# First block of a two-block layer stack: the order of turning, scoring and the fourth input product, and the place of two modulation rows on VectorE

## The chip, the cores and the metric

The kernel runs on one core of one Trainium2 chip. The metric is the device time of one execution in microseconds (us), as the median of several runs. Three runs of the kernel before took 3032.94, 3033.38 and 3045.9 us; the median is 3033.38 us.

## What is computed

The reference is two blocks, each of two layers, on 256 tokens of width 1024. The change touches only the attention part of the first block, in both of its layers:

```python
mod = (c_act @ w_ada[l] + b_ada[l])[:, None, :]
shift1, scale1, gate1, shift2, scale2, gate2 = jnp.split(mod, 6, axis=-1)
h = rms_norm(x, norm1_g[l]) * (1.0 + scale1) + shift1
z = h @ w_in[l]          # q 512, k 128, v 128, conv_x/b/c 3*256, pool_x 256
q = partial_rope(rms_norm(q, q_norm_g[l]), cos, sin)
k = partial_rope(rms_norm(k, k_norm_g[l]), cos, sin)
attn_o = windowed_gqa(q, k, v, attn_sink[l])       # 8 query heads, 2 key heads, a sink
conv_o = conv_b * short_conv(conv_c * conv_x, conv_w[l])
pooled = multiscale_pool(pool_x)
pool_o = jnp.einsum('bsgc,gce->bsge', pooled, pool_w[l]).reshape(b, s, POOL_WIDTH) * pool_scale[l]
mix = jnp.concatenate([attn_o, conv_o, pool_o], axis=-1) @ w_out[l]
x = x + gate1 * mix
h2 = rms_norm(x, norm2_g[l]) * (1.0 + scale2) + shift2
x = x + gate2 * peer_ffn(...)       # 16384 experts: most of the first block's time
```

The second block (three kinds of attention and an MLP, two layers) follows, and is not touched.

## The kernel before

Each engine has a program of its own, written out by hand. The engines meet at semaphores: `wait_ge` stands in an engine's queue, and all that is queued behind it on that engine waits too. All data are float32. The 256 tokens are two tiles (t) of 128 partitions.

**The input product** z = h @ w_in is cut into four slabs of weights, `in0` (queries), `in1` (keys, values, first conv part), `in2` (the rest of conv) and `in3` (the 256 columns of pooling), each a product on TensorE (PE) into one of the two halves of the PSUM tensor `acc` and then copied out by ScalarE (ACT) with `keep_acc`. The halves of `acc` are dealt out in the fixed order of the list `ACCS_A` (line 174), and a use waits until the use before it in the same half has been copied out. The order is in0, in1, in2, in3, sc0, sc1, sc2, sc3, then out0 and so on.

**Ahead of attention.** VectorE (DVE) normalizes and rotates queries and keys (lines 2594 to 2605) as soon as in0 and in1 are copied out, while PE is still at `in2`. PE runs `gemm_T` of in2 (line 1186, timed at L973), the product in3 (lines 1187 to 1195, L1193), and then turns q0, q1 and k (transposes, L1027), which ACT copies to SBUF (in the second layer DVE copies q1). Then come `score(0)` (L1096), the pooling product `pool0` (L1210), `score(1)`, and `pool1` (L1221), which needs ACT's copy of pool0.

**Attention** goes over four groups g of heads. For each: `score(g)` on PE; `masked(g)` on DVE (scale and mask out of PSUM L2450, maximum L2455, and three small operations); `exps(g)` on ACT (L1783, L1785); `turn_probs(g)` on PE (L1107) in two halves, one copied by ACT and one by DVE in `sums(g)` (L2472, L2474, and the copy at L1658); `values(g)` on PE (L1122); `attended(g)` on DVE (L2501), which frees the bank. DVE does masked(0), masked(1), and then for each g: sums(g), masked(g + 2) while there is one (for g = 2 `convolved()` instead, L2615 to L2625), attended(g). ACT runs pool1's scaling (L1863), exps(1), and then for each g its half of the copy and exps(g + 2).

**Rows of modulation.** In the first layer the 12 pieces of 512 columns of c_act @ w_ada are not all computed at the start. `ada_first(s)` on DVE (L2415, L2422) adds up one of them from four loaded pieces in eight operations on 128x512, and PE sums the partitions with a product by ones, `ada_added(s)` (L1137). ada_first(3) and ada_first(4) stand behind the rotation and ahead of masked(0). PE takes their sums, ada_added(3) and (4), only after values(3), and their results are needed after the output product.

**Loads.** SyncE (SP) issues all weight loads, in this order: slab in3, the pieces of rows 3 and 4, slabs out0 and out1, the pieces of rows 5, 6, 7, slab wq0 and so on. A piece of row s waits until the same piece of row s - 1 has been used by DVE (`ada_used`, L685). The load of out1 waits for in3's product to be done.

After attention PE runs ada_added(3), ada_added(4), the turns `mix0` and `mix1` of the attention output, and the output product out0 (L952).

Of the kernel before, what the change touches and what calls it, by code (L numbers as in the profile page):

```python
# [19 lines left out]
T = S // P  # L20
# [136 lines left out]
def spread(ap, axis, n):  # L157
# [13 lines left out]
         + [f"br{c}" for c in range(NB)] + ["wo0", "wo1"] + [f"up{i}" for i in range(8)]  # L171
         + [f"dn{i}" for i in range(8)],
}
ACCS_A = [f"in{i}" for i in range(4)] + [f"sc{i}" for i in range(4)]
ACCS_A += ["out0", "out1", "wq0", "s0", "wq1", "s1", "wq2", "s2", "wq3", "s3"]
ACCS = {
    "a": (["ada2", "ada3", "ada0", "ada1"] + ACCS_A, ACCS_A),
    "b": ["dq", "dk", "sc0", "dv", "sc1", "mq", "sc2", "mk", "sc3", "mv", "sc4", "misc0", "sc5", "misc1",
# [62 lines left out]
def two_blocks(nc, io, out):  # L241
    ctx = ExitStack()
    with ctx:
        def sem(name):
            return ctx.enter_context(nc.semaphore(name))
# [47 lines left out]
        qk_ready = Signal(sem("qk_ready"), a=1, b=4)  # L293
# [158 lines left out]
        z = ra.take(T, D)  # L452
# [156 lines left out]
        def qpair(t, j):  # L609

            return z[:, t, j * P:j * P + P]
# [335 lines left out]
        def _(pe):  # L947
# [28 lines left out]
            def gemm_T(block, l, use):  # L976
                w = w8(block, use)
                pe.wait_ge(*slabs.full_at(block, l, use))
                pe.wait_ge(*accs.free_at(block, l, use))
                for j in range(4):  # L980
                    ins = columns_T(acc[:, accs.buf(block, use), j, :], w, hT, j * P)
                ins.then_inc(accs.full_sem(block, use), 1)
# [39 lines left out]
            def turn(block, l, use, blocks, rows=P):  # L1022

                ring, bank = turned_bank(block, use)
                pe.wait_ge(*ring.free_at(block, l, use))
                for i, src in enumerate(blocks):
                    ins = pe.transpose(bank[0:rows, i * P:i * P + P], src, ident[:])  # L1027
                ins.then_inc(ring.full_sem(block, use), 1)
# [55 lines left out]
            def wait_turned(block, l, *uses):  # L1084

                for u in uses:
                    pe.wait_ge(*(probs if u in PROBS[block] else turns).emptied_at(block, l, u))

            def score(block, l, g):
                d = group(block, g)  # L1090
                use = f"sc{g}"
                pe.wait_ge(*accs.free_at(block, l, use))
                b = accs.buf(block, use)
                for hh in range(2):
                    for t in range(T):
                        ins = pe.matmul(acc[:, b, 2 * hh + t, :], d["q"](hh, t), d["k"](hh), start=True, stop=True)  # L1096
                ins.then_inc(accs.full_sem(block, use), 1)
# [35 lines left out]
            for l in range(DEPTH):  # L1133
# [49 lines left out]
                if l == 0:  # L1183
                    ada_added(1, prob_ps[:, 0])
                    ada_added(2, prob_ps[:, 1])
                gemm_T("a", l, "in2")
                pe.wait_ge(*slabs.full_at("a", l, "in3"))
                pe.wait_ge(*accs.free_at("a", l, "in3"))
                w = w8("a", "in3")
# [4 lines left out]
                                        start=(k == 0), stop=(k == KD - 1))  # L1194
                ins.then_inc(accs.full_sem("a", "in3"), 1)

                pe.wait_ge(*qk_ready.at("a", l, 1))
                for n in range(2):
                    turn("a", l, f"q{n}", [qpair(t, 2 * n + c) for c in range(2) for t in range(T)])
                turn("a", l, "k", [z[:, t, 512:640] for t in range(T)])  # L1200
                wait_turned("a", l, "q0", "q1", "k")
                score("a", l, 0)

                pe.wait_ge(*accs.emptied_at("a", l, "in3"))
                pe.wait_ge(*turns.free_at("a", l, "pool0"))
                pooled = turn_ps[:, turns.buf("a", "pool0"), :].rearrange("p (c s) -> p c s", c=2)
# [3 lines left out]
                        ins = pe.matmul(pooled[r:r + 64, g // 2, :], z[:, kt, 768 + 64 * g:832 + 64 * g],  # L1210
                                        pool_m[:, kt, g, :], start=(kt == 0), stop=(kt == 1))
                ins.then_inc(turns.full_sem("a", "pool0"), 1)
                score("a", l, 1)
                pe.wait_ge(*turns.emptied_at("a", l, "pool0"))
                pe.sem_inc(passed["pe"], 1)
                pe.wait_ge(*turns.free_at("a", l, "pool1"))
# [200 lines left out]
                else:  # L1417
# [3 lines left out]
                    with pe.Fori(0, 12) as it:  # L1421
                        for j in range(8):
                            i = it * 8 + (PLAIN + 3 + j)
# [211 lines left out]
        def keep_turned(eng, block, l, use, dst, rows=P, n=512):  # L1635

            ring, bank = turned_bank(block, use)
            eng.wait_ge(*ring.full_at(block, l, use))
            src = bank[0:rows, 0:n]
            if len(dst.shape) == 3:  # L1640
                src = src.rearrange("p (k s) -> p k s", k=dst.shape[1])
            copy(eng, dst, src).then_inc(ring.free_sem(block, use), 1)
# [75 lines left out]
        def _(act):  # L1718
# [9 lines left out]
            def keep_acc(block, l, use, *pairs):  # L1728

                act.wait_ge(*accs.full_at(block, l, use))  # L1730
                for dst, src in pairs[:-1]:
                    act.copy(dst, src)
                act.copy(*pairs[-1]).then_inc(accs.free_sem(block, use), 1)
# [4 lines left out]
            def whole(block, use):  # L1738
                return acc[:, accs.buf(block, use)]
# [38 lines left out]
            def exps(block, l, g):  # L1778

                act.wait_ge(*sm_ready.at(block, l, g + 1))  # L1780
                s = sm_of(block)
                if block == "a":
                    act.activation(esink[:, g % 2], esink[:, g % 2], ACT.Exp)  # L1783
                for u in range(4):
                    ins = act.activation(s[:, g % 2, u], s[:, g % 2, u], ACT.Exp, bias=nm[:, g % 2, u:u + 1],  # L1785
                                         accum_out=den[:, g % 2, u:u + 1])
                ins.then_inc(p_ready.sem, 1)
# [36 lines left out]
            for l in range(DEPTH):  # L1824
# [25 lines left out]
                    for s in (1, 2):  # L1850
                        ada_copied(s, mod_flat[:, 512 * ADA_ORDER[s]:512 * ADA_ORDER[s] + 512], prob_ps[:, (s - 1) % 2])
                keep_acc("a", l, "in2", (zT[:, 2:6], whole("a", "in2")))
                keep_acc("a", l, "in3", (z[:, :, 768:1024], whole("a", "in3")[:, 0:2]))
                keep_turned(act, "a", l, "q0", qT[:, 0:2])
                if l == 0:
                    keep_turned(act, "a", l, "q1", qT[:, 2:4])
                keep_turned(act, "a", l, "k", kT, n=S)
                keep_turned(act, "a", l, "pool0", plT)
                exps("a", l, 0)
                act.wait_ge(*turns.full_at("a", l, "pool1"))  # L1860
                pooled = turn_ps[:, turns.buf("a", "pool1"), :].rearrange("p (c s) -> p c s", c=2)
                for c in range(2):
# [474 lines left out]
        def _(dve_):  # L2337
# [84 lines left out]
            def ada_first(s):  # L2422

                for p in range(4):
                    if p == 0:
                        if s >= 3:
                            dve.wait_ge(ada_out, s - 2)
                        dve.wait_ge(bias_row_in, 16 * s)
                    ada_piece(s, p, start_pieces, ada_acc[:, s % 2], bias_row)
                dve.drain().then_inc(ada_sum, 1)  # L2430
# [13 lines left out]
            def masked(block, l, g):  # L2444

                d, s, use = group(block, g), sm_of(block), f"sc{g}"
                dve.wait_ge(*accs.full_at(block, l, use))
                b = accs.buf(block, use)
                for hh in range(2):
                    ins = dve.scalar_tensor_tensor(s[:, g % 2, 2 * hh:2 * hh + 2].rearrange("p t s -> p (t s)"),  # L2450
                                                   acc[:, b, 2 * hh:2 * hh + 2].rearrange("p t s -> p (t s)"), d["scale"],
                                                   d["mask"](hh).rearrange("p t s -> p (t s)"), ALU.mult, ALU.add)
                ins.then_inc(accs.free_sem(block, use), 1)
                dve.drain()
                dve.tensor_reduce(mx, s[:, g % 2], X, ALU.max)  # L2455
                dve.drain()
                if block == "a":
                    sink = spread(sinks.rearrange("p (hh j) -> p j hh", hh=2)[:, g], 2, T)
                    mx2, es2, nm2 = (v.rearrange("p (hh t) -> p hh t", t=T) for v in (mx, esink[:, g % 2], nm[:, g % 2]))
                    dve.tensor_tensor(mx2, mx2, sink, ALU.max)  # L2460
                    dve.drain()
                    dve.tensor_scalar(nm[:, g % 2], mx, -1.0, None, ALU.mult)
                    dve.drain()
                    dve.tensor_tensor(es2, nm2, sink, ALU.add).then_inc(sm_ready.sem, 1)
                else:
                    dve.tensor_scalar(nm[:, g % 2], mx, -1.0, None, ALU.mult).then_inc(sm_ready.sem, 1)
# [80 lines left out]
            for l in range(DEPTH):  # L2547
# [55 lines left out]
                dve.drain()  # L2603
                rt = [rope_t[:, i].rearrange("p t (h e) -> p t h e", e=8) for i in range(4)]
                rotate(heads[:, :, :, 0:8], heads[:, :, :, 8:16], cosA, sinA, rt).then_inc(qk_ready.sem, 1)
                if l == 0:
                    ada_first(3)
                    ada_first(4)
                else:
                    keep_turned(dve, "a", l, "q1", qT[:, 2:4])  # L2610

                def convolved():
# [13 lines left out]

                masked("a", l, 0)
                masked("a", l, 1)
                for g in range(4):
                    sums("a", l, g)  # L2630
                    if g + 2 < 4:
                        masked("a", l, g + 2)
                    elif g == 2:
                        convolved()
                    attended("a", l, g)
# [161 lines left out]
                else:  # L2797
# [6 lines left out]
                    with dve.Fori(0, 12) as it:  # L2804
                        for j in range(8):
                            i = it * 8 + (PLAIN + 3 + j)
# [365 lines left out]
```

## Time and profile before

| | |
|---|---|
| median of three runs | 3033.38 us |
| the profiled execution | 3034.02 us, span 3032.2 us |
| mean granted TensorE clock | 0.987 |
| first layer, from the start of in3 to the start of out0 | 84.0 to 131.6 us |
| second layer, the same | 1120.0 to 1164.5 us |

The profile shows one execution. Times in the trace are counted from the start of the span. A row of a timeline has start, duration, engine, line and operation, output and input with shapes, the number of instructions merged into it, and in brackets how long the engine was idle before it and what released it. The granted clock is 1.00 at 2.4 GHz and 0.50 at 1.2 GHz.

### The profile page before, as it was taken

What the parts mean: (1) busy time and instruction counts of PE and PEld (TensorE: products, weight loads), DVE (VectorE), ACT (ScalarE), POOL (GpSimd) and SP (SyncE); (2) the same over time, 40 slices, a digit from 0 to 9 for tenths busy, and PEclk for the clock granted to TensorE, in tenths of its full rate; (3) what the DMA queues carried; (4) which work ended last, traced back from release to release, by engine and by line L of the source; (5) the groups of instructions that cost most, each with busy time, mean ns of one, the idle gap of its engine ahead of it and who ended that gap; (6) DMA issues with size and microseconds to landing.
All of it is one profiled execution on the core that took longest, in us unless ns stands there. A gap on an engine that the chain in (4) does not pass through costs nothing.

```text
span 3032.2 us, 49210 instructions
## 1 busy us (share of the span) xinstructions
PE 2937.6 (97%) x17378; PEld 2555.9 (84%) x17378; DVE 1970.5 (65%) x3639; ACT 1308.6 (43%) x2110; POOL 274.5 (9%) x398
## 2 busy tenths in 40 slices
PE   8899999999999999999999999998999999999999
PEld 4686989999999876887999999998977888878897
DVE  4759966777777633898666666666556654655664
ACT  1245834444444412575444444444443433533433
POOL 0026700000000000572000000000000000000000
PEclk9899999999999998999999999999999999999999
DMA  8542256666666641404555555554334454324454
GB/s 327 197 157 84 72 187 235 226 235 232 227 234 230 206 155 56 167 8 128 192 186 186 198 191 194 190 194 176 125 120 168 171 185 172 147 112 160 153 181 153
DMA packets 130815, 524.41 MB, mean 173 GB/s; under 512 B 17981, under 2 KB 28093, under 8 KB 108025
## 3 DMA queue, kind: packets, MB, share of 16 engines
q1 hardware_dynamic: 120648, 508.13, 48.4%
q10 hardware_dynamic: 10034, 14.52, 1.4%
q8 instruction: 81, 1.33, 0.2%
q14 instruction: 52, 0.43, 0.0%
HBM read 519.44 MB, written 3.16 MB: 172 GB/s over the span
## 4 chain that ended last, share of the span: by engine, by line
PE 86%; DVE 7%; ACT 4%; issue 1%; DVEq 1%; DMA 1%; ACTq 0%; POOL 0%; SPq 0%
PE acc L1390 23%; PE prob_ps L1378 21%; PE acc L1014 7%; PE acc L1603 6%; PE acc L1616 6%; PE acc L999 3%; PE acc L973 2%; PE acc L1550 2%; PE acc L1360 2%; PE turn_ps L1122 2%; PE acc L952 2%; PE prob_ps L1341 2%; PE acc L1575 1%; PE acc L1096 1%; PE acc L1253 1%
## 5 line engine op out<-in xcount | busy, mean ns | idle before, releaser
L1378 PEld LDWEIGHTS prob_ps<-hTr,utr 128*128 128x128 f32 x5472 | 686.3, 191 | 19.6 <-issue 2.0
L1378 PE MATMUL prob_ps<-hTr,utr 128*128 128x256 f32 x5472 | 692.3, 283 | 1.3 <-issue 1.1
L1390 PE MATMUL acc<-vr,wtr 128*128 128x512 f32 x2736 | 663.6, 391 | 0.2 <-DVE vr L2776 0.2
L1390 PEld LDWEIGHTS acc<-vr,wtr 128*128 128x128 f32 x2736 | 499.3, 188 | 94.9 <-issue 0.6
L2776 DVE TENSOR_TENSOR vr<-slab,vr 128x1024 fp32r<-128x1024 f32 x228 | 279.3, 1225 | 357.9 <-ACT vr L2036 357.9
L2036 ACT CAST vr<-slab 128x1024 fp32r<-128x1024 f32 x228 | 239.5, 1050 | 524.1 <-PE acc L1390 524.0
L2751 DVE TENSOR_TENSOR utr<-slab,utr 128x1024 fp32r<-128x1024 f32 x228 | 277.9, 1219 | 16.1 <-ACT utr L2003 16.1
L2305 POOL TENSOR_TENSOR small<-small 128x1 f32<-128x1 f32 (+4 forms) x29 | 26.2, 902 | 2610.3 <-DVE small L2368 1410.5
L2003 ACT CAST utr<-slab 128x1024 fp32r<-128x1024 f32 x228 | 238.6, 1047 | 16.6 <-DMA slab<-in_peer_u 10.5
L3032 DVE TENSOR_TENSOR slab_lo<-slab,w_hi 128x2048 fp32r<-128x2048 f32 x64 | 143.8, 2288 | 123.0 <-ACT w_hi L2271 123.0
L2271 ACT CAST w_hi<-slab 128x2048 fp32r<-128x2048 f32 x64 | 119.3, 1907 | 158.5 <-DMA slab<-in_pack_b 150.6
L2027 ACT ACTIVATE arena<-prob_ps 128x256 f32<-128x256 f32 x228 | 87.6, 384 | 194.1 <-PE prob_ps L1378 194.1
L2857 DVE TENSOR_TENSOR slab_r<-slab,arena_r 128x2048 fp32r<-128x2048 f32 (+1 forms) x52 | 115.7, 2258 | 84.5 <-ACT arena_r L2123 84.4
L973 PE MATMUL acc<-hT,slab 128*128 128x256 f32 x704 | 157.7, 379 | 2.9 <-ACT hT L1652 2.9
L1616 PE MATMUL acc<-w_hi,uTr 128*128 128x512 f32 x512 | 157.8, 389 | 2.3 <-issue 2.3
L2328 POOL TENSOR_SCALAR slab<-iota,arena 128x128 f32<-128x128 f32 x256 | 152.2, 609 | 45.0 <-ACT arena L1658 30.5
L2740 DVE TENSOR_SCALAR slab<-iota,arena 128x128 f32<-128x128 f32 x512 | 152.7, 367 | 1.2
L973 PEld LDWEIGHTS acc<-hT,slab 128*128 128x128 f32 x704 | 131.5, 190 | 21.1 <-issue 3.7
L1360 PEld LDWEIGHTS acc<-slab 128*128 128x128 f32 x1024 | 121.7, 192 | 19.1 <-DVE slab L2744 15.7
L1360 PE MATMUL acc<-slab 128*128 128x128 f32 x1024 | 127.1, 277 | 6.9 <-ACT slab L1984 4.2
L2415 DVE SCALAR_TENSOR_TENSOR arena<-arena,small 128x512 f32<-128x512 f32 x152 | 113.8, 749 | 15.7 <-DMA arena<-in_pack_a 7.4
L1014 PE MATMUL acc<-arena_r,hT_hi 128*128 128x512 f32 (+2 forms) x320 | 122.3, 382 | 0.0
(314 smaller groups left out, 4415.4 us busy)
## 6 DMA issues: line engine op xcount, KB each, us to landing
slab<-in_pack_b SPq DMA_DIRECT2D x132, 1024.0 KB, 4.8
slab<-in_peer_v SPq DMA_DIRECT2D x256, 512.0 KB, 3.5
slab<-in_peer_u SPq DMA_DIRECT2D x244, 512.0 KB, 4.5
arena<-in_pack_a SPq DMA_DIRECT2D x84, 512.0 KB, 4.8
slab<-in_pack_a SPq DMA_DIRECT2D x40, 1024.0 KB, 6.9
arena<-in_peer_u SPq DMA_DIRECT2D x6, 1024.0 KB, 15.1
slab<-in_pack_b SPq DMA_DIRECT2D x4, 832.0 KB, 5.6
arena<-in_pack_a SPq DMA_DIRECT2D x2, 1024.0 KB, 18.6
```

What stands on the lines that cost most here:

```text
L973: ins = pe.matmul(dst, w(k, a, P), lhs[:, k, :], start=(k == 0), stop=(k == KD - 1))
L1014: ins = pe.matmul(dst[:, t, 0:n], hT_r[hp][:, 4 * h + k, t * P:t * P + P], proj_operand(u0 + h, wp)[:, k, a:a + n], start=(h == 0 and k == ...
L1360: ins = pe.matmul(gate_ps[:, n % 2, q * P:q * P + P], rows[:, n % 2, 1, q, :], rows[:, n % 2, 0, q, :], start=True, stop=True)
L1378: ins = pe.matmul(prob_ps[:, m % 2, 0:S], utr[:, m % 2, uh, k * P:k * P + P], hTr[:, hh, k, :], start=(k == 0 and n == 0), stop=(k == KD - ...
L1390: ins = pe.matmul(y_ps[:, t, n, :], wtr[:, m % 2, wh, t * P:t * P + P], v[:, vh, n * 512:n * 512 + 512], start=first and k == 0, stop=last ...
L1603: ins = pe.matmul(acc[:, accs.buf("b", use), 2 * h + j, :], mlp_operand(u, wp)[:, k, j * P:j * P + P], hm_r[hp][:, k, :], start=(k == 0 an ...
L1616: ins = pe.matmul(acc_nat(accs.buf("b", f"dn{n}"))[:, t, :], uTr[:, up, 4 * j + k, t * P:t * P + P], mlp_operand(u, wp)[:, k, :], start=(j ...
L2003: act.copy(utr[:, m % 2, 0], expert_u[:, m % 2]).then_inc(ut_act.sem, 1)
L2036: act.copy(v_place(l, i)[:, 0], v_raw(l, i, m)).then_inc(v_hi.sem, 1)
L2740: dve.tensor_scalar(rows[:, n % 2, 0, q, :], iota[:], pairsT[:, 0, tok:tok + 1], pairsT[:, 2, tok:tok + 1], ALU.is_equal, ALU.mult)
L2751: dve.tensor_tensor(utr[:, m % 2, 1], expert_u[:, m % 2], utr[:, m % 2, 0].bitcast(F32), ALU.subtract).then_inc(ut_dve.sem, 1)
L2776: dve.tensor_tensor(v_hl[:, 1], v_raw(l, i, m), v_hl[:, 0].bitcast(F32), ALU.subtract)\
```

## The change

On PE, turning q0, q1 and k and score(0) move ahead of the product in3, and score(1) moves ahead of pool0. The order of the halves of `acc` follows: sc0 now comes ahead of in3. On ACT, exps(0) moves ahead of the copy of in3 and of pool0. This holds for both layers. On DVE, in the first layer only, ada_first(3) moves behind masked(1) and ada_first(4) behind masked(3).

```diff
-ACCS_A = [f"in{i}" for i in range(4)] + [f"sc{i}" for i in range(4)]
+ACCS_A = ["in0", "in1", "in2", "sc0", "in3"] + [f"sc{i}" for i in range(1, 4)]
...
                 gemm_T("a", l, "in2")
+                pe.wait_ge(*qk_ready.at("a", l, 1))
+                for n in range(2):
+                    turn("a", l, f"q{n}", [qpair(t, 2 * n + c) for c in range(2) for t in range(T)])
+                turn("a", l, "k", [z[:, t, 512:640] for t in range(T)])
+                wait_turned("a", l, "q0", "q1", "k")
+                score("a", l, 0)
+
                 pe.wait_ge(*slabs.full_at("a", l, "in3"))
                 pe.wait_ge(*accs.free_at("a", l, "in3"))
...
                 ins.then_inc(accs.full_sem("a", "in3"), 1)
 
-                pe.wait_ge(*qk_ready.at("a", l, 1))
-                for n in range(2):
-                    turn("a", l, f"q{n}", [qpair(t, 2 * n + c) for c in range(2) for t in range(T)])
-                turn("a", l, "k", [z[:, t, 512:640] for t in range(T)])
-                wait_turned("a", l, "q0", "q1", "k")
-                score("a", l, 0)
-
+                score("a", l, 1)
                 pe.wait_ge(*accs.emptied_at("a", l, "in3"))
...
                 ins.then_inc(turns.full_sem("a", "pool0"), 1)
-                score("a", l, 1)
                 pe.wait_ge(*turns.emptied_at("a", l, "pool0"))
...
                 keep_acc("a", l, "in2", (zT[:, 2:6], whole("a", "in2")))
-                keep_acc("a", l, "in3", (z[:, :, 768:1024], whole("a", "in3")[:, 0:2]))
                 keep_turned(act, "a", l, "q0", qT[:, 0:2])
                 if l == 0:
                     keep_turned(act, "a", l, "q1", qT[:, 2:4])
                 keep_turned(act, "a", l, "k", kT, n=S)
+                exps("a", l, 0)
+                keep_acc("a", l, "in3", (z[:, :, 768:1024], whole("a", "in3")[:, 0:2]))
                 keep_turned(act, "a", l, "pool0", plT)
-                exps("a", l, 0)
...
-                if l == 0:
-                    ada_first(3)
-                    ada_first(4)
-                else:
+                if l:
                     keep_turned(dve, "a", l, "q1", qT[:, 2:4])
...
                 masked("a", l, 0)
                 masked("a", l, 1)
+                if l == 0:
+                    ada_first(3)
                 for g in range(4):
                     sums("a", l, g)
                     if g + 2 < 4:
                         masked("a", l, g + 2)
+                        if l == 0 and g == 1:
+                            ada_first(4)
                     elif g == 2:
                         convolved()
                     attended("a", l, g)
```

## Rows read from the trace of the kernel before

**Rows 1.** The page: busy time of the engines; the last chain by engine.

```profile
PE 2937.6 (97%) x17378; PEld 2555.9 (84%) x17378; DVE 1970.5 (65%) x3639; ACT 1308.6 (43%) x2110; POOL 274.5 (9%) x398
PE 86%; DVE 7%; ACT 4%; issue 1%; DVEq 1%; DMA 1%; ACTq 0%; POOL 0%; SPq 0%
```

**Rows 2.** The chain that ended last, first layer: start, us, what.

```profile
94.51 0.75 DVE arena L2415
...
95.45 0.69 DVE arena L2450
...
108.47 1.71 PE prob_ps L1107 x8
```

**Rows 3.** Timeline, first layer, PE and ACT.

```profile
84.04 7.07 PE L1193 MATMUL acc<-slab,hT 128*128 128x256 f32 x32
84.24 1.01 ACT L1733 COPY arena<-acc 128x1024 f32<-128x1024 f32 x1 [13.23 <-PE acc L973]
...
90.94 1.04 PE L1027 MATMUL turn_ps<-ident,arena 128*128 128x128 f32 x8
91.14 0.59 ACT L1733 COPY arena<-acc 128x512 f32<-128x512 f32 x1 [5.89 <-PE acc L1193]
91.62 1.49 ACT L1658 COPY arena<-turn_ps 128x512 f32<-128x512 f32 x3
...
93.37 1.14 PE L1096 MATMUL acc<-arena 64*128 64x256 f32 x8 [0.67 <-ACT arena L1658]
94.44 2.00 PE L1210 MATMUL turn_ps<-arena 128*64 128x256 f32 x16
...
101.08 1.18 PE L1107 MATMUL prob_ps<-ident,arena 128*128 128x128 f32 x8 [2.55 <-issue]
...
126.69 3.19 PE L1137 MATMUL prob_ps<-arena,small 128*128 128x512 f32 x4
...
129.71 1.04 PE L1027 MATMUL turn_ps<-ident,arena 128*128 128x128 f32 x8
...
131.58 13.97 PE L952 MATMUL acc<-slab,arena 128*128 128x512 f32 x32 [0.83 <-ACT arena L1658]
```

**Rows 4.** Timeline, first layer, DVE.

```profile
81.82 6.57 DVE L2415 SCALAR_TENSOR_TENSOR arena<-arena,small 128x512 f32<-128x512 f32 x8
...
98.69 1.28 DVE L2450 SCALAR_TENSOR_TENSOR arena<-acc,arena 128x512 f32<-128x512 f32 x2
...
115.48 0.48 DVE L2501 TENSOR_TENSOR arena<-turn_ps,small 128x128 f32<-128x128 f32 x2
...
116.78 0.68 DVE L2615 TENSOR_TENSOR arena<-arena 128x512 f32<-128x512 f32 x1
...
120.15 0.69 DVE L2625 TENSOR_TENSOR arena<-arena 128x512 f32<-128x512 f32 x1
...
126.93 0.49 DVE L2501 TENSOR_TENSOR arena<-turn_ps,small 128x128 f32<-128x128 f32 x2 [2.87 <-PE turn_ps L1122]
```

**Rows 5.** Windows of 1 us, first layer; the granted clock follows the engines.

```profile
101.00:102.00 1.00, 0.92 (x8) 0.85 (x8) 0.78 (x4) 0.70 (x2) 0.00 (x0) 0.94 0.98 412
...
129.00:130.00 1.00, 1.00 (x5) 0.43 (x4) 0.00 (x0) 0.42 (x2) 0.00 (x0) 0.90 0.00 0
```

**Rows 6.** Timeline, second layer, PE.

```profile
1119.97 7.07 PE L1193 MATMUL acc<-slab,hT 128*128 128x256 f32 x32
...
1136.53 1.09 PE L1107 MATMUL prob_ps<-ident,arena 128*128 128x128 f32 x8 [0.20 <-ACT arena L1785]
...
1139.93 1.97 PE L1122 MATMUL turn_ps<-arena 128*128 128x64 f32 x16 [1.24 <-ACT arena L1658]
...
1157.42 3.65 PE L1122 MATMUL turn_ps<-arena 128*128 128x64 f32 x16
...
1164.50 16.83 PE L952 MATMUL acc<-slab,arena 128*128 128x512 f32 x32 [0.83 <-issue]
```

**Rows 7.** SP's queue, first layer: issue of out0 and out1.

```profile
88.94 3.50 SPq L668 DMA_DIRECT2D slab<-in_pack_a  x4
```

## The prediction

> **What bounds the kernel now.** I read the page first: PE is busy 97% of the span and holds 86% of the chain that ended last; DVE holds 7% [rows 1]. A move can win only where that chain leaves PE, so I followed the chain through the attention of both layers of the first block. In the first layer it lies on DVE's modulation rows until 95.26, and then on masked(0) at 95.45 [rows 2]. There the reader is to see the target: DVE is through with the rotation at 81.82 and spends the 13.63 us to 95.45 on two rows of two times eight operations [rows 2, 4], and only then masks scores that PE finished at 94.51 (93.37 + 1.14) [rows 3]. So before the change the rows cost at most 0.94 us: that is how late masked(0) is behind its scores. The timelines of PE, ACT and DVE then give the durations, and the windows the clock: TensorE stands at 2.4 GHz up to 101.9 us, drops to 1.2 GHz inside the window at 101, just behind PE's idle stretch of 2.55 us, and is back for good inside the window at 129, with one return in between [rows 3, 5].
>
> **PE's new order, first layer.** PE is free at 84.04 [rows 3]; the queries have been ready since 81.8, so the turns start at once. ACT must first copy in2 (84.24, 1.01 us); a next copy starts 0.11 us before the one ahead of it ends (91.14 + 0.59 against 91.62) [rows 3], so with the hand-over the copy of q0 starts at about 85.15. From that copy's start to score(0) took 1.75 us (91.62 to 93.37) and takes it again: score(0) at 86.9, next work 1.07 later at 87.97, then in3, 6.90 us (84.04 to 90.94): score(1) starts at 94.87 and is done at 96.01 [rows 3]. masked(0) then starts at 88.04, 7.4 us earlier, and with exps(0) is wholly hidden beside in3. But masked(1) waits for score(1) at 96.03, where it started at 98.69 [rows 4]: only **2.66 us** of the 7.4 reach the next step. DVE is idle for about 6 us ahead of score(0) and 4.8 between masked(0) and score(1), and the rows are no longer there to use it.
>
> **PE's stalls.** pool1 now follows pool0 with no score between, so PE waits for ACT's copy (about 0.6 us with the hand-over, from the copies in rows 3). turn_probs(0) can start at about 99.5 instead of 101.08 [rows 3]. That gain dies at once: values(0) needs DVE's half of the copy, in sums(0), which is queued behind ada_first(3).
>
> **DVE's new order, first layer.** From 96.03 DVE has, end to end: three masks of 3.24 us (95.45 to 98.69) = 9.72 [rows 2, 4]; two rows of 6.81 (13.63 / 2) = 13.62; four sums and three attended, of which one pair takes 1.30 (115.48 to 116.78) and attended alone about 0.40, = 4.80; the convolution 4.06 (116.78 to 120.84) = 4.06 [rows 4]. That is 32.20 us: 128.2. What can make it wait? attended(0) finds values(0) done. masked(3) waits for score(3): PE can start the second half of values(0) at 107.0, and at 1.2 GHz needs 1.83 (half of the 3.65 of a values group), 1.71 for the turn and twice 1.07 for the score [rows 2, 3, 6]: 112.6, against DVE ready at 111.5, so 1.1 us; at 2.4 GHz nothing. I take the slow clock, since the trace had it at this place, from 101.9 on [rows 5]: **129.3**. Then the second half of values(3), 1.83 us: PE is through at 131.1, where it was at 126.69 [rows 3]. Where 13.6 us of rows were nearly free, they now stand in the chain, less the waits that DVE had in attention and the 2.66 us.
>
> **From there to out0.** ada_added(3) and (4) are four passes of 512 columns; one takes 13.97 / 32 = 0.43 us at 2.4 GHz, twice that at 1.2, so 3.4 us (before, with the clock rising within them, 3.02: 126.69 to 129.71). The two turns take 1.04 at 2.4 GHz or twice that, then 0.83 of wait [rows 3]. With the clock back at the turns, out0 starts at 136.4, with it back after them at 137.3; before it was 131.58. That is +4.8 or +5.7, and I take **+5.2**. Bounds: all of it at 2.4 GHz gives 128.2 + 1.0 + 1.7 + 1.0 + 0.8 = 132.7, +1.2; a clock that comes back only within out0, as in the second layer, where out0 took 16.83 instead of 13.97 us [rows 3, 6], gives +5.7 + 2.9 = +8.6.
>
> **Second layer.** It has no rows to move. PE is free for the turns at 1119.97 [rows 6]. By the same steps: q0's copy at 1121.08, score(0) at 1122.8, in3 to 1130.8, score(1) to 1131.9, pool0 to 1133.9, the copy 0.6, pool1 to 1135.5, gain2 to 1137.4: turn_probs(0) starts 0.9 us later than 1136.53 [rows 6]. masked(0) was not late here for DVE's sake; ACT's exps(0) ended 0.2 us before PE took it up, so starting it 6 us earlier is worth 0.2. exps(1) stands on ACT behind the copy of gain2, which follows PE: values(0) at 1140.4 instead of 1139.93 [rows 6]. The rest follows in step: **+0.5**, between 0 and +0.9 without the clock. The clock may fall one step later, because the dense product in3 ends 4 us later: up to 1.7 us back.
>
> **What moves at no cost.** SP: the pieces of row 4 now wait for ada_first(3)'s, so the loads of out0 and out1, issued from 88.94 [rows 7], go out at about 106.1. 17 us later, but out0 is needed at 136.4: cover of 30 us. The pieces of row 5 wait for ada_first(4) (115.5 to 122.3) and are needed by ada_first(5) after the mix turns, some 13 us later. out1's load waits for in3's product, later by 4 us, with the same cover. in3 waits for in2's copy in its half of acc, done at 85.3; score(1) waits for masked(0)'s read, done at 89.3. The exp table load on ACT goes with exps(0) into the idle time beside in3.
>
> **Sum.** +5.2 + 0.5 = +5.7 on the profiled 3034.02 us, which is 0.64 above the median of the runs: 3039.1 us; I say 3039.
>
> **Rivals.**
> 1. *The clock holds* (not slower). The change takes away the idle stretch ahead of turn_probs(0), just where the clock fell [rows 3, 5]. If it then stays at 2.4 GHz, the first layer costs +1.2; if the second layer's attention too stays fast, values fall from 3.65 to 1.97 us three times and out0 from 16.83 to 13.97 [rows 6], some 8 to 10 us with the turns. That gives 3025 to 3034. Against it: ada_first(3) opens new idle stretches on PE, about 2 and 2.5 us around the first half of values(0), and ada_first(4) one of some 4 us ahead of the second half of values(2). The Trainium skill, "TensorE: Matmul & The Clock Gate", Part 1, has it that dense work releases the throttle and gaps bring it back; by it the dense stretch moved to 95 us speaks for this case and the new gaps against it. [...]
> 2. *The clock is lost for longer*: low until within out0, +8.6 and +0.9: 3043.
> 3. *out0's weights come late* (slower by over 0.5%). Their load would have to take over 30 us from its issue at 106; each further us is a us. 15 us more would be needed to reach 3049.
> 4. *The change does as its order suggests*: DVE's idle time swallows the rows. In attention DVE waited some 9.0 us in all between 102 and 127, in eight places, the largest the 2.87 us ahead of attended(3) [rows 4]. 13.6 - 2.66 - 9.0 leaves 1.9 even if every wait were filled, and the last one can't be, since values(3) itself must run: it is the case of 3035 to 3036, not a gain.
>
> **Chances.** Forecast (3036.5 to 3042) 0.57; rival 1, 0.14; rival 2 (3042 to 3046), 0.16; rival 3, 0.03; rival 4, 0.10. Range 3031 to 3046.5: it takes in the slow-clock bound and the upper half of rival 1, leaving out some 0.15. A measurement of this kernel tells about 0.5% (15 us) from no change: that is 3018 to 3048.5. Nearly all cases lie within it: same 0.93, slower 0.05, faster 0.02.
>
> **What would show it.** After, in the first layer: masked(0) near 88 and masked(1) near 96; ada_first(3) from 99 to 106 with PE idle; values(0) finished near 109; ada_first(4) near 115.5 to 122; values(3) ending near 131 and out0 starting near 137. The chain there should lie on L2415 again, for 13 us, now within attention. out0's slab should be issued near 106 with no wait of PE for it. Second layer: turn_probs(0) about 0.9 us later against in3's old start. Wrong would be: a clock at 1.00 from 102 to 112; masked(1) well before 96; PE waiting for a DMA at out0.

## The result

| | before | after |
|---|---|---|
| median, 20 runs each | 3035.32 us | 3042.15 us |
| profiled execution | 3034.02 us | 3039.9 us |
| span | 3032.2 us | 3038.1 us |

The changed kernel is slower by a little: the ratio is 1.0023, with a 95% interval of 1.0015 to 1.0032, or 4.6 to 9.7 us. That is within the 0.5% that the prediction took as the least it could tell from no change; 20 runs of each kernel tell more. The forecast was 5.7 us more than before; measured are 6.8 between the medians and 5.9 between the two profiled executions. Executions in a slower state (two of the twelve of e5, for one) are left out of all ratios. The page counts the same instructions and the same busy time of PE to 0.1 us as before [rows 1]. The 5.9 us between the spans are therefore time in which PE stood idle.

The page of the changed kernel:

```profile
PE 2937.6 (97%) x17378; PEld 2555.5 (84%) x17378; DVE 1970.8 (65%) x3639; ACT 1309.2 (43%) x2110; POOL 275.4 (9%) x398
```

The timeline of the changed kernel, first layer, PE:

```profile
84.17 1.04 PE L1027 MATMUL turn_ps<-ident,arena 128*128 128x128 f32 x8
...
87.02 1.14 PE L1096 MATMUL acc<-arena 64*128 64x256 f32 x8 [0.66 <-ACT arena L1658]
88.09 7.17 PE L1200 MATMUL acc<-slab,hT 128*128 128x256 f32 x32
...
95.19 1.14 PE L1096 MATMUL acc<-arena 64*128 64x256 f32 x8
...
100.19 1.09 PE L1107 MATMUL prob_ps<-ident,arena 128*128 128x128 f32 x8
...
107.51 1.97 PE L1122 MATMUL turn_ps<-arena 128*128 128x64 f32 x8 [2.63 <-DVE arena L1658]
...
124.41 1.97 PE L1122 MATMUL turn_ps<-arena 128*128 128x64 f32 x8 [3.44 <-DVE arena L1658]
...
137.45 10.97 PE L952 MATMUL acc<-slab,arena 128*128 128x512 f32 x25 [0.83 <-ACT arena L1658]
```

And DVE of the same stretch, with SP's issue of out0 and out1 (L1200 and L1211 are now the lines of in3 and pool0):

```profile
88.20 1.29 DVE L2450 SCALAR_TENSOR_TENSOR arena<-acc,arena 128x512 f32<-128x512 f32 x2 [6.15 <-PE acc L1096]
...
96.39 1.29 DVE L2450 SCALAR_TENSOR_TENSOR arena<-acc,arena 128x512 f32<-128x512 f32 x2 [4.87 <-PE acc L1096]
...
99.69 6.59 DVE L2415 SCALAR_TENSOR_TENSOR arena<-arena,small 128x512 f32<-128x512 f32 x8
...
106.82 2.62 SPq L668 DMA_DIRECT2D slab<-in_pack_a  x4
...
112.89 1.29 DVE L2450 SCALAR_TENSOR_TENSOR arena<-acc,arena 128x512 f32<-128x512 f32 x2 [0.55 <-PE acc L1096]
...
116.19 6.60 DVE L2415 SCALAR_TENSOR_TENSOR arena<-arena,small 128x512 f32<-128x512 f32 x8
```

The reader is to see two things. DVE waits 6.15 us ahead of masked(0) and 4.87 us ahead of masked(1), where it had work before [rows 4]. Then it does 6.6 us of row 3 (99.69 to 106.28) ahead of sums(0), while PE gets through the first half of values(0), and 6.6 us of row 4 ahead of attended(1) and sums(2). Twice PE's values stop half done for DVE's half of the copy (2.63 us in values(0), 3.44 us in values(2)). Before, the first layer's stretch from PE free of in2 to the start of out0 was 131.58 - 84.04 = 47.54 us [rows 3]; now it is 137.45 - 84.17 = **53.28 us**. That stretch is the measure of the experiments.

### The profile page after: what moved, and what is told of

Its sections match the earlier page's. It is cut to its first block, busy times and chain, and to the rows that moved or that the text cites. A ratio compares the mean times of both kernels' runs of the same rounds, so it can differ in the third digit from the quotient of the medians.

```text
span 3038.1 us, 49210 instructions
## 1 busy us (share of the span) xinstructions
PE 2937.6 (97%) x17378; PEld 2555.5 (84%) x17378; DVE 1970.8 (65%) x3639; ACT 1309.2 (43%) x2110; POOL 275.4 (9%) x398
## 4 chain that ended last, share of the span: by engine, by line
PE 87%; DVE 6%; ACT 3%; issue 1%; DMA 1%; DVEq 1%; ACTq 0%; SPq 0%; POOL 0%
PE acc L1390 23%; PE prob_ps L1378 22%; PE acc L1014 7%; PE acc L1603 6%; PE acc L1616 6%; PE acc L999 3%; PE acc L973 3%; PE acc L1550 2%; PE acc L1360 2%; PE acc L952 2%; PE turn_ps L1122 2%; PE prob_ps L1341 2%; PE acc L1575 1%; PE acc L1096 1%; DMA arena<-in_pack_a 1%
```

## The experiments

The stretch is read from one profiled execution of each kernel, between two starts of PE's rows in its timeline. The ratio is over many executions (12 of each experiment), against runs of the kernel before taken beside them. The edit of e2 is shown against the kernel before, the others against the changed kernel.

| kernel | stretch, us | ratio to before (95% interval) |
|---|---|---|
| before, before_again | 47.54, 47.35 | |
| after, after_again | 53.28, 52.92 | 1.0023 (1.0015 to 1.0032) |
| e1_order_only | 55.19 | 1.0022 (1.0012 to 1.0032) |
| e2_rows_only | 54.60 | 1.0015 (1.0003 to 1.0026) |
| e4_thin_rows | 44.50 | 0.9989 (0.9978 to 1.0000) |
| e3_fill, e3_again | 38.44, 44.62 | 0.9993 (0.9981 to 1.0006), 1.0003 (0.9991 to 1.0015) |
| e5_both_scores | 46.81 | 0.9994 (0.9982 to 1.0005) |
| e6_order_pe | 49.70 | none: one run, 3042.70 us, against one of before, 3033.12 us |

before_again and after_again are one run each too (3042.34 and 3043.92 us). The 20 runs of the kernel before lie between 3028.93 and 3045.9 us, so a single run says nothing of a difference of some us.

### e4: the moved rows without their length

Here n is 8 for rows 3 and 4: the other 504 columns of these two rows are left out, so this kernel only serves to measure.

```diff
-    ins = dve.scalar_tensor_tensor(total, pieces[:, p, k], ...
+    ins = dve.scalar_tensor_tensor(total[:, 0:n], pieces[:, p, k, 0:n], ...
```

> The changed kernel with rows 3 and 4 computed for 8 of their 512 columns only (the rest of these two rows is left out): the same instructions, waits and loads, without their length. Theory: each row falls from 6.8 to about 1.5 us, and 10.6 us leave DVE's chain, of which PE gives back some: stretch 44 to 46 us. Rival (the loads and waits that hang on the rows, or the order, cost): the stretch stays above 50 us. Total: theory 5 to 9 us below the changed kernel.

The stretch fell from 53.28 to 44.50 us, and the ratio to before from 1.0023 to 0.9989: 0.34%, some 10 us, where 5 to 9 were expected. Waits, loads and order are those of the changed kernel; only the length of the rows on DVE is gone. So in this place the length of the rows costs 8.8 us of the stretch, and neither their loads nor their waits do. That another place is cheaper in the same order is for e3 to show.

### e2: the rows moved, the order as before

ada_first(4) stands behind masked(3).

```diff
-                if l == 0:
-                    ada_first(3)
-                    ada_first(4)
-                else:
+                if l:
                     keep_turned(dve, "a", l, "q1", qT[:, 2:4])
...
                 masked("a", l, 1)
+                if l == 0:
+                    ada_first(3)
```

> The old order on PE and ACT, with the two rows behind masked(1) and masked(3). Theory: masked(0) starts at 94.5 with its scores, masked(1) at 97.8, 1.4 us later than in the changed kernel, and the whole chain of DVE follows it: stretch 54 to 55 us, total 6 to 9 us above before. Rival (the order is the cost): stretch about 48 us, total as before.

The stretch is 54.60, as the theory had it. The whole is 1.0015, or 4.6 us with an interval of 0.9 to 7.9, against 6 to 9 expected. The timeline of e2 on DVE shows the shift:

```profile
94.58 1.29 DVE L2450 SCALAR_TENSOR_TENSOR arena<-acc,arena 128x512 f32<-128x512 f32 x2 [12.63 <-PE acc L1096]
97.82 1.28 DVE L2450 SCALAR_TENSOR_TENSOR arena<-acc,arena 128x512 f32<-128x512 f32 x2
101.11 6.61 DVE L2415 SCALAR_TENSOR_TENSOR arena<-arena,small 128x512 f32<-128x512 f32 x8
```

DVE idles for 12.63 us, and masked(0) starts only 0.87 us earlier than the 95.45 of before [rows 2]. In the old order the rows had held up the masks by 0.9 us where they were.

### e1 and e6: the order alone

Both rows go back ahead of the masks, and none stands behind masked(1) or masked(3).

```diff
                 rotate(heads[:, :, :, 0:8], ...).then_inc(qk_ready.sem, 1)
+                if l == 0:
+                    ada_first(3)
+                    ada_first(4)
```

> The new order on PE and ACT, both layers, with the two modulation rows back ahead of masked(0). The measure is the first layer's stretch from PE free of in2 to the start of out0: before 47.5 us, after 53.3 us. Theory (the moved rows are the cost): masked(0) waits for the rows again and starts at 95.5, masked(1) at 98.7, and the stretch is 47.5 us, within 1 us. Rival (the new order itself costs, by PE's stall ahead of pool1 and the later masked(1)): 51 to 53 us. In the second layer both expect the same stretch as after, 42.7 us against 44.5 before. Total: theory within 3 us of before, rival 4 to 6 us above.

The theory's 47.5 us was wrong, and so was its reading of the order as harmless. The stretch is 55.19 us, more than with the whole change and more than the 51 to 53 of the rival. The timeline of e1, PE, ACT and DVE:

```profile
95.43 1.29 DVE L2450 SCALAR_TENSOR_TENSOR arena<-acc,arena 128x512 f32<-128x512 f32 x2 [0.19 <-issue]
...
96.78 1.14 PE L1096 MATMUL acc<-arena 64*128 64x256 f32 x8 [1.68 <-DVE arena L2450]
...
100.86 0.56 ACT L1733 COPY arena<-acc 128x512 f32<-128x512 f32 x1
...
101.48 3.73 PE L1211 MATMUL turn_ps<-arena 128*64 128x256 f32 x16 [3.56 <-ACT arena L1733]
```

In the new order score(1) shares a half of acc with score(0) and waits for masked(0) to read it (1.68 us), and ACT's copy of in3 stands behind exps(0), which waits for masked(0). With the rows ahead of masked(0), that copy came at 100.86, and PE stood for 3.56 us ahead of pool0. In that wait the granted clock fell (0.83 in the window at 100, 0.50 from 101): pool0 took 3.73 us, where it takes 2.00 in the changed kernel, and pool1 1.97 instead of 1.08. e6 takes the second of the two away:

```diff
-                exps("a", l, 0)
                 keep_acc("a", l, "in3", (z[:, :, 768:1024], whole("a", "in3")[:, 0:2]))
                 keep_turned(act, "a", l, "pool0", plT)
+                exps("a", l, 0)
```

> As e1_order_only, but exps(0) on ACT goes back behind the copies of in3 and pool0. In e1 the copy of in3, queued behind exps(0), which waited for a masked(0) held up by the rows, came at 100.9 and held PE's pool0 until 101.5. Theory (that place in ACT's queue made e1 slow): the copy at about 95.5, score(1) at 96.8 still behind masked(0)'s read, pool0 at 97.9, turn_probs(0) near 101.5, and a stretch of 47.5 to 49 us. Rival (the shared half of acc, by which score(1) waits for masked(0), made it slow): 52 us or more.

The timeline of e6:

```profile
95.08 0.58 ACT L1733 COPY arena<-acc 128x512 f32<-128x512 f32 x1 [8.54 <-PE acc L1200]
```

pool0 followed at 97.80, and the stretch was 49.70: 5.5 us of e1's 7.7 over before are gone, and the stretch is 0.7 us above the top of what was expected. The 5.5 us hold the clock too: some 2.6 of them are the slow pool0 and pool1 of e1 (3.73 - 2.00 and 1.97 - 1.08), which followed on the wait. turn_probs(0) started at 104.00, not 101.5, since pool0's copy and the exp table load now stood ahead of exps(0) on ACT. So the place in ACT's queue made most of e1's slowness; the shared half of acc costs the 1.7 us ahead of score(1).

So the halves of the change do not add: the order alone is worth +7.7 us in this stretch (55.19 against the mean of before, 47.45), the rows alone +7.1, both together +5.7 (53.10). Moving the rows is what lets exps(0) run early enough not to hold in3's copy; it then costs about as much elsewhere. These three differences come from one execution of e1 and of e2 and from means of two of before and after, and the clock fell at other moments in each; the ratios (1.0022, 1.0015 and 1.0023) agree that none of the three is a gain, and do not rank them.

### e3: the rows where DVE is idle

Of row 4, three of its four pieces go between the masks, and the last ahead of attended(3).

```diff
+                if l == 0:
+                    ada_first(3)
                 masked("a", l, 0)
+                if l == 0:
+                    ada_first(4, range(3))
                 masked("a", l, 1)
-                if l == 0:
-                    ada_first(3)
...
                     elif g == 2:
                         convolved()
+                    elif l == 0:
+                        ada_first(4, range(3, 4))
                     attended("a", l, g)
```

> The new order, with row 3 ahead of masked(0), three of the four pieces of row 4 between masked(0) and masked(1), and the last piece ahead of attended(3): the rows stand where DVE is idle in the new order. Theory: masked(0) starts at 88.7, masked(1) at 96.9, and the 2 us that masked(1) is earlier than before carry through: stretch 45 to 46.5 us, 1 to 2.5 us less than before. Rival (the order costs): 51 us or more. Total: theory 0 to 3 us below before, if the clock falls as before.

> The same kernel as e3_fill. Its first profile had the whole of the first layer's attention at 2.4 GHz and out0 at 123.0. Theory (the places of the rows give 2 to 3 us, the clock the rest, and the clock holds in some executions only): out0 between 123 and 129.5 depending on the clock; over many runs 1 to 4 us less than before. Rival (the order with filled gaps keeps the clock up always): out0 at 123 again and 6 us or more below before.

The stretch was 38.44 us in the first execution and 44.62 in the second, of the same program: 9.0 and 2.8 us below before's mean. Expected were 45 to 46.5, so both came out shorter than the theory. Both are the same row for row up to the second values, and part at the third. First e3_fill, then e3_again, PE's timeline:

```profile
114.34 1.97 PE L1122 MATMUL turn_ps<-arena 128*128 128x64 f32 x16 [2.51 <-ACT arena L1658]
116.15 1.04 PE L1107 MATMUL prob_ps<-ident,arena 128*128 128x128 f32 x8
...
122.97 13.97 PE L952 MATMUL acc<-slab,arena 128*128 128x512 f32 x32 [0.83 <-ACT arena L1658]
```

```profile
113.80 3.48 PE L1122 MATMUL turn_ps<-arena 128*128 128x64 f32 x16 [2.51 <-ACT arena L1658]
117.07 1.91 PE L1107 MATMUL prob_ps<-ident,arena 128*128 128x128 f32 x8
...
128.60 11.83 PE L952 MATMUL acc<-slab,arena 128*128 128x512 f32 x27 [0.83 <-issue]
```

The wait ahead of values(2) is 2.51 us in both. In one the products behind it take 1.97 us (2.4 GHz), in the other 3.48 and then 3.65 (1.2 GHz). The rival, a clock that is always kept, is out. Over 12 runs each, the two rounds give 0.9993 and 1.0003, both intervals across 1: the 3 us of the place are not shown as a gain of the whole against before, and the 1 to 4 us expected of e3_again were not found. Against the changed kernel's 1.0023 the same order with filled gaps is faster, by 6 to 9 us between the ratios. Together with e4 this shows the cause: in the new order the same two rows at full length cost the stretch 8.5 us (53.10 against 44.62) or more behind masked(1) and masked(3) than in the gaps. In the gaps they cost next to nothing: 44.62 us with full rows against 44.50 with thinned ones, both with the clock at 1.2 GHz from the third values on (in e4 also around score(3), 2.09 us against 1.14).

### e5: both scores ahead of in3

The order of the scores is shown; besides, exps(1) follows in3's copy on ACT, and of the eight pieces of the rows three stand ahead of masked(0), four behind masked(1) and one ahead of attended(3).

```diff
-ACCS_A = ["in0", "in1", "in2", "sc0", "in3"] + [f"sc{i}" for i in range(1, 4)]
+ACCS_A = ["in0", "in1", "in2", "sc0", "sc1", "in3", "sc2", "sc3"]
...
                 score("a", l, 0)
+                score("a", l, 1)
```

> A candidate: as e3_fill, but score(1) too stands ahead of in3 (its own half of acc, in3 behind masked(0)), exps(1) on ACT follows in3's copy, and the rows stand as three pieces ahead of masked(0), four behind masked(1), one ahead of attended(3). Theory (DVE's chain from masked(1) on is what ends last): masked(1) ends at about 95 instead of 100, values(0) starts at about 102.5 instead of 104.2, and out0 starts 1.5 to 2.5 us earlier than in e3_fill at the same clock; 3 to 6 us below before over many runs. Rival (PE's own order bounds it by now): the same as e3_fill within 1 us.

The timeline of e5, PE:

```profile
89.49 7.14 PE L1201 MATMUL acc<-slab,hT 128*128 128x256 f32 x32 [0.54 <-DVE arena L2451]
...
101.24 1.09 PE L1107 MATMUL prob_ps<-ident,arena 128*128 128x128 f32 x8
...
109.66 3.65 PE L1122 MATMUL turn_ps<-arena 128*128 128x64 f32 x16 [2.38 <-ACT arena L1658]
```

The theory fell. values(0) started at 103.33, against 103.62 in e3_again. DVE had masked both groups by 94.5, as expected, but PE now waited for masked(0) ahead of in3 (0.54 us), for ACT ahead of pool0 (0.68) and for pool0's copy (0.92), and turn_probs(0) came at 101.24 instead of 100.02. Up to values(0) PE's own order is the bound, as the rival said. Behind it the clock was at 1.2 GHz from 109.5 to 129.3, where it fell at 114 in e3_again, and the stretch was 46.81: longer by 2.2 us, not the same within 1 us. The ratio shows no gain (0.9994, 0.9982 to 1.0005).

### before_again and after_again: the same programs once more

> The kernel before, unchanged, in a second profiled execution. Theory (engines other than PE repeat to a tenth of a us, and what differs between executions is when TensorE's clock falls and rises): the first layer's stretch up to 101 us repeats within 0.2 us, and behind it the stretches at 1.2 GHz begin at other moments, so that the whole may differ by up to 10 us. Rival (an execution is repeatable and the differences between kernels outside the changed part come from the change): the same places and lengths at 1.2 GHz as in the first profile.

> The changed kernel, unchanged, in a second profiled execution. Theory: DVE's chain from masked(1) to attended(1) repeats within 0.3 us (96.4 to 123.4), since no clock of PE is in it but for score(3); the start of out0 moves by the clock alone, between 133.5 and 139. Rival (repeatable): out0 at 137.45 again within 0.2 us.

Windows over the first and the second layer's attention, granted clock as the third number from the right. Before, before_again, after, after_again:

```profile
90.00:160.00 70.00, 61.67 (x247) 38.53 (x246) 43.56 (x82) 20.59 (x60) 0.56 (x1) 0.85 0.51 189
1100.00:1230.00 130.00, 121.43 (x564) 92.88 (x563) 53.30 (x163) 33.45 (x102) 4.63 (x3) 0.91 0.24 89
```

```profile
90.00:160.00 70.00, 60.58 (x247) 38.09 (x246) 43.97 (x82) 20.70 (x60) 0.56 (x1) 0.88 0.52 191
1100.00:1230.00 130.00, 122.26 (x537) 93.30 (x536) 48.88 (x132) 31.45 (x94) 4.64 (x3) 0.86 0.24 89
```

```profile
90.00:160.00 70.00, 57.33 (x234) 37.77 (x233) 47.22 (x86) 16.94 (x53) 0.00 (x0) 0.83 0.58 209
1100.00:1230.00 130.00, 119.90 (x562) 90.99 (x562) 50.08 (x139) 32.71 (x98) 4.64 (x3) 0.92 0.26 97
```

```profile
90.00:160.00 70.00, 57.37 (x234) 37.63 (x234) 47.56 (x87) 16.94 (x53) 0.00 (x0) 0.83 0.58 210
1100.00:1230.00 130.00, 121.51 (x536) 92.30 (x535) 46.20 (x114) 27.87 (x75) 4.64 (x3) 0.87 0.24 90
```

The first layer repeats to 0.4 us or better in its stretch, whatever the moments of the clock: DVE's chain from masked(1) (96.28 in after_again) to attended(1) (122.63) is 26.35 us, against 26.58, and out0 started at 136.98: inside the theory's bounds, but with a stretch only 0.36 us off the first one, so that this pair of executions hardly sets the theory apart from the rival. The pair of before does. Behind the idle stretch ahead of turn_probs(0), 2.55 and 2.58 us long, the clock fell within the window at 101 in the first execution [rows 5] and only in the one at 106 in the second:

```profile
101.00:102.00 1.00, 0.55 (x5) 0.58 (x6) 0.85 (x3) 1.00 (x4) 0.00 (x0) 1.00 0.97 410
...
106.00:107.00 1.00, 1.00 (x10) 1.00 (x10) 0.75 (x4) 0.00 (x0) 0.00 (x0) 0.83 1.01 393
```

The second layer does not repeat. From PE free of in2 to out0 it took 44.53 and 49.92 us in the two executions of before, and 42.68 and 49.24 in those of after. Some 5 to 7 us of either kernel's time there depend on when the clock falls. Single profiled executions are therefore no measure of the second layer, and the difference of 5.9 us between the two profiles agrees with the medians in part by luck: out0 of the first layer was 5.87 us late, the second layer's start 3.59 (1123.56 against 1119.97), its out0 1.74 (1166.24 against 1164.50), and the end 5.9 again. Most of the last 4 us arose behind the attention that was changed, and no run says why.

## Why the prediction was right

**The order on PE and the two waits of DVE.** Forecast and measured: score(0) 86.9 and 87.02, score(1) 94.87 and 95.19, masked(0) 88.04 and 88.20, masked(1) 96.03 and 96.39, turn_probs(0) 99.5 and 100.19. PE was free 0.13 us later than in the trace of before, and the steps came at most another 0.6 us late. Two terms were too short: in3 took 7.10 us (88.09 to 95.19) instead of 6.90, and PE waited 0.92 us for pool0's copy instead of 0.6. The early masked(0) was hidden beside in3, as said, and the gain at turn_probs(0) died at values(0).

**The rows in DVE's chain.** ada_first(3) was forecast at 99.3 and started at 99.69; ada_first(4) was forecast at 115.8 and started at 116.19; masked(3) waited for score(3) until 112.89 (forecast 112.6). e4 shows what they cost: without their length the stretch is 8.8 us shorter.

**The step that was wrong in kind.** The sum ran DVE's chain on through sums(2), the convolution, attended(2) and sums(3) to 129.3 and then added half of values(3): 131.1. DVE was through with them at 129.62:

```profile
128.96 0.66 DVE L1658 COPY arena<-prob_ps 128x512 f32<-128x512 f32 x1
```

The trace has values(3) end at 131.44 for another reason. The chain that ended last, changed kernel:

```profile
124.41 1.97 PE turn_ps L1122 x8
126.38 1.71 PE prob_ps L1107 x8
128.09 3.56 PE turn_ps L1122 x16
131.65 3.52 PE prob_ps L1137 x4
```

It leaves DVE at the copy in sums(2). From there PE's second half of values(2), the turn and all of values(3) at 1.2 GHz, 7.24 us, were the longer branch; the convolution and sums(3) ran beside them. PE was through with the first half of values(3) at about 129.9 (128.09 and half of 3.56), some 0.3 us after DVE's copy was there, so the number held although the last part of its chain was not the longer branch. That the two were so close was luck.

**From there to out0.** The four passes of the sums took 3.52 us at 1.2 GHz (forecast 3.4). The clock rose within the turns, which took 1.65 us; then PE was idle for 0.83 us. out0 started at 137.45, just above both forecasts, 136.4 and 137.3 (the second one's own terms, 131.1 + 3.4 + 2.1 + 0.8, give 137.4). Against before the stretch grew by 5.74 us where +5.2 was taken.

**The second layer.** The term was +0.5, between 0 and +0.9 without the clock. Its steady part came out at the upper end of that, and the spread by the clock was missed. Up to the start of values(1), all at 2.4 GHz, before took 1145.98 - 1119.97 = 26.01 us and after 1150.46 - 1123.56 = 26.90. First the row of before, then those of the changed kernel:

```profile
1145.98 3.36 PE L1122 MATMUL turn_ps<-arena 128*128 128x64 f32 x16 [0.26 <-ACT small L1658]
```

```profile
1123.56 1.04 PE L1027 MATMUL turn_ps<-ident,arena 128*128 128x128 f32 x8
...
1141.39 1.07 PE L1107 MATMUL prob_ps<-ident,arena 128*128 128x128 f32 x8
...
1150.46 2.00 PE L1122 MATMUL turn_ps<-arena 128*128 128x64 f32 x16 [0.26 <-ACT small L1658]
```

e1_order_only and e4_thin_rows, with the same order there, have 26.92 and 26.91: +0.9. The whole stretch, expected at 42.7 us in e1, was 45.76 there (1125.29 to 1171.05), since the clock fell at values(1). The forecast had turn_probs(0) 0.9 late; it was 1.3 late (1141.39 - 1123.56 = 17.83 against 16.56 [rows 6]), by the same two terms as in the first layer: in3 took 7.10 us instead of 6.90 (1127.48 to 1134.58), and pool1 waited 0.92 instead of 0.6. The clock behind it is worth 5 to 7 us of either kernel's stretch, from one execution to the next; the term allowed 1.7 back. In the two profiles themselves the second layer's stretch got shorter, 42.68 against 44.53 us. It is therefore in part luck that the sum of +5.2 and +0.5 meets the +5.9 of the profiles; what the trace bears out is the first layer's +5.7.

**The time in us.** The forecast of 3039 stood on the median of three runs, 3033.38 us. Over 20 runs before is at 3035.32, so 1.9 of the 3.1 us between 3039 and the measured 3042.15 lie in the median of before. 3042.15 is 0.15 above the band given to the forecast (3036.5 to 3042), in that of rival 2, but rival 2's mechanism is not what the trace shows: the clock was back before out0 (0.89 in the window at 136, 1.00 in the next).

**The rivals.** The clock did not hold in the changed kernel. It fell within the window at 105, in the wait of 2.63 us that row 3 made, was back within the one at 112, and stood at 1.2 GHz again from 119 to 136:

```profile
105.00:106.00 1.00, 0.00 (x0) 0.00 (x0) 0.93 (x2) 0.00 (x0) 0.00 (x0) 0.75 0.80 217
...
112.00:113.00 1.00, 0.83 (x6) 0.35 (x4) 0.45 (x2) 1.00 (x5) 0.00 (x0) 0.84 1.06 401
...
119.00:120.00 1.00, 0.91 (x5) 0.94 (x5) 0.91 (x2) 0.00 (x0) 0.00 (x0) 0.57 0.94 387
...
136.00:137.00 1.00, 0.61 (x5) 0.38 (x3) 0.35 (x1) 0.59 (x1) 0.00 (x0) 0.89 0.00 0
```

The prediction weighed what the Trainium skill, "TensorE: Matmul & The Clock Gate", Part 1, has of gaps that bring the throttle back. The changed kernel's trace agrees in so far as its clock fell in the wait of 2.63 us and again behind the one of 2.67 us ahead of values(2), at 119.09; e3_fill and e3_again show that it does not settle one execution, since one kept the clock and the other lost it with the same 2.51 us of gap at the place where they part. Rival 1's clock is thus real, but for another place of the rows: with them out of PE's way the whole attention of the first layer ran at 2.4 GHz, in one execution, and was 6.2 us shorter than in the other. The premise of rival 1, that the idle stretch ahead of turn_probs(0) is where the clock falls, is weak as well: in before_again the clock stayed up behind it for 5 us. The weights of out0 were issued at 106.82 (forecast 106.1), and PE did not wait for them at 137.45, so rival 3 is out. For rival 4, DVE's idle time did not take up the rows.

## What to carry to other kernels

When work of PE is pulled ahead, look at what the engine that follows it does with the time: here masked(0) started 7.3 us earlier, masked(1) 2.3, and the two long rows that had filled DVE's idle time were moved behind the point where DVE is busy. Long filler belongs into the new gap (ahead of masked(0) and between the masks), not behind it; here that took back what the change cost, and no gain over the kernel before is shown. And a new order changes which use shares a buffer and what stands behind a wait: try each half of such a change alone, since the halves here cost 7.7 and 7.1 us and together 5.7.

## What was not expected of the hardware

The same program got another clock in another execution: e3_fill and e3_again part at the third values with the same 2.51 us of wait ahead of it, and their stretches differ by 6.2 us. The second layer of the unchanged kernel took 44.53 or 49.92 us, with the mean granted clock of the window 0.91 or 0.86. The kernel before ranged from 3028.93 to 3045.9 us in 20 runs, and the interval over 20 runs of each still spans 5 us. What sets the moment at which the clock falls was not tested. e3's place of the rows is shorter in the stretch in both executions and not shown to be faster in the whole; that stays open.
